# Where the last three steps of a unit's expert selection stand in VectorE's unit loop

## What is computed

```python
v1, i1 = lax.top_k(s1, PEER_TOPK)
v2, i2 = lax.top_k(s2, PEER_TOPK)
cand = (v1[..., :, None] + v2[..., None, :]).reshape(-1, PEER_HEADS, PEER_TOPK * PEER_TOPK)
sc, ci = lax.top_k(cand, PEER_TOPK)
e1 = jnp.take_along_axis(i1, ci // PEER_TOPK, axis=-1)
e2 = jnp.take_along_axis(i2, ci % PEER_TOPK, axis=-1)
eidx = e1 * N_KEYS + e2
gate = jax.nn.softmax(sc, axis=-1)
z = jax.nn.gelu(jnp.einsum('cd,chkd->chk', hc, u_tab[eidx]), approximate=False)
coef = (gate * z.astype(jnp.float32)).astype(hc.dtype)
return jnp.einsum('chk,chkd->cd', coef, v_tab[eidx])
```

## Time and profile before

| | us |
|---|---|
| median of 3 runs | 2758.37 |
| lowest, highest run | 2747.98, 2760.15 |
| the profiled execution | 2752.55 |
| its span (first to last instruction) | 2750.8 |
| DVE busy | 1364.6 (50%) |
| ACT busy | 1031.9 (38%) |
| POOL busy | 1311.3 (48%) |
| PE busy | 1985.1 (72%), granted clock 0.712 of full speed on average |

### The profile page before, as it was taken

One profiled execution on the slowest core, in us unless ns is written; L12 is line 12 of the kernel. 1 busy time (PEld: TensorE's weight loads), 2 busy tenths in 40 slices (PEclk: granted clock), 3 DMA queues, 4 the chain that ended last, 5 costly groups with the idle time before them and its releaser, 6 DMA issues.

```text
span 2750.8 us, 32207 instructions
## 1 busy us (share of the span) xinstructions
PE 1985.1 (72%) x10179; PEld 1594.1 (58%) x10179; DVE 1364.6 (50%) x3386; ACT 1031.9 (38%) x1308; POOL 1311.3 (48%) x1216
## 2 busy tenths in 40 slices
PE   6998865666666665698589897898656666666666
PEld 3676754544545544576389896567444555455455
DVE  1032655465655655323752624726465656556552
ACT  2202344444444444513211111223444444454545
POOL 2000677777777777300000000006777777777774
PEclk8899965565555555799689897899656555555556
DMA  9743899999999999724100002427999999999996
GB/s 359 289 153 124 287 363 329 361 365 367 337 360 351 367 360 392 293 95 168 38 1 1 1 1 76 115 67 249 350 347 361 351 372 347 360 362 364 356 351 243
DMA packets 242654, 717.42 MB, mean 261 GB/s; under 512 B 39672, under 2 KB 45056, under 8 KB 242556
## 3 DMA queue, kind: packets, MB, share of 16 engines
q0 software_dynamic: 165888, 604.05, 59.4%
q1 hardware_dynamic: 62212, 105.00, 10.9%
q10 hardware_dynamic: 14456, 7.06, 1.0%
HBM read 712.38 MB, written 3.65 MB: 260 GB/s over the span
## 4 chain that ended last, share of the span: by engine, by line
PE 35%; DMA 18%; issue 17%; DVE 13%; POOL 10%; ACT 6%; POOLq 0%; DVEq 0%; ACTq 0%; SPq 0%
PE ps L557 14%; DMA ARENA<-in_peer_v,CURV 13%; POOL ARENA L1872 10%; DVE ARENA L1449 7%; PE ps L646 5%; PE ps L774 5%; DMA ARENA<-in_peer_u,CURU 3%; ACT ARENA L1114 2%; ACT L1064 1%; PE ps L534 1%; PE ps L756 1%; PE ps L520 1%; DMA W<-in_w_ada 1%; PE ps L510 1%; PE ps L619 1%
## 5 line engine op out<-in xcount | busy, mean ns | idle before, releaser
L646 PE MATMUL ps<-ident,ARENA 128*128 128x128 f32 x4608 | 1023.3, 398 | 617.5 <-ACT ARENA L1114 616.6
L646 PEld LDWEIGHTS ps<-ident,ARENA 128*128 128x128 f32 x4608 | 833.4, 209 | 807.5 <-ACT ARENA L1114 788.3
L1872 POOL DMA_INDIRECT ARENA<-in_peer_u,CURU x576 | 642.2, 1115 | 1174.2 <-DVE ARENA L1424 978.2
L1114 ACT ACTIVATE ARENA<-ARENA,CF 128x1024 f32<-128x1024 f32 x576 | 658.1, 1147 | 769.8 <-DMA ARENA<-in_peer_v,CURV 766.6
L1449 DVE SCALAR_TENSOR_TENSOR ARENA<-ARENA 128x1024 f32<-128x1024 f32 x576 | 686.6, 1223 | 185.1 <-DMA ARENA<-in_peer_u,CURU 183.5
L1872 POOL DMA_INDIRECT ARENA<-in_peer_v,CURV x576 | 653.1, 1134 | 230.6 <-issue 152.3
L557 PE MATMUL ps<-H,W 128*128 128x288 f32 x1024 | 255.0, 412 | 3.5 <-DVEq L1801 2.8
L1429 DVE TENSOR_REDUCE gsm<-ARENA 128x1 f32<-128x16 f32 x36 | 6.1, 170 | 472.5 <-ACT ARENA L1064 472.5
L557 PEld LDWEIGHTS ps<-H,W 128*128 128x128 f32 x1024 | 197.7, 194 | 58.8 <-DVEq L1801 3.0
L967 ACT ACTIVATE W<-ps 128x512 f32<-128x512 f32 (+2 forms) x97 | 55.8, 577 | 231.4 <-PE ps L774 171.4
L967 ACT ACTIVATE ARENA<-ps 128x512 f32<-128x512 f32 (+4 forms) x106 | 55.0, 541 | 201.7 <-PE ps L557 85.2
(11 more groups left out here) (282 smaller groups left out, 1657.6 us busy)
## 6 DMA issues: line engine op xcount, KB each, us to landing
W<-in_w_ada SPq DMA_DIRECT2D x24, 2048.0 KB, 12.6
W<-in_peer_wq SPq DMA_DIRECT2D x8, 2048.0 KB, 8.2
W<-in_conv_w_in SPq DMA_DIRECT2D x6, 2048.0 KB, 12.3
ARENA<-in_peer_u,CURU POOLq DMA_INDIRECT x576, 6.3
ARENA<-in_peer_v,CURV POOLq DMA_INDIRECT x576, 6.2
W<-in_conv_w_out SPq DMA_DIRECT2D x2, 2048.0 KB, 7.9
W<-in_rwkv_wr SPq DMA_DIRECT2D x2, 2048.0 KB, 24.0
W<-in_rwkv_wk SPq DMA_DIRECT2D x2, 2048.0 KB, 10.4
```

What stands on the lines that cost most here:

```text
L646: m = pe.matmul(ps[:, acc + c // 4, c % 4 * P:(c % 4 + 1) * P], RVV[:, k % RING, c * P:(c + 1) * P], ident[:], start=(first and k == 0 and ...
L1114: act.activation(RVV[:, k % RING, :], RVV[:, k % RING, :], ACT.Copy, scale=CF[:, e, k:k + 1]).then_inc(s_scaled, 1)
L1872: pool.indirect_dma_start(ring[:, k % RING, :], None, tab, bass.IndirectOffsetOnAxis(ap=idx[:, k:k + 1], axis=0)).then_inc(landed[k % RING ...
```

## The change

DVE's unit loop asks for the pieces of the selection at other rows. Before, rows 1 to 7 run two pieces each, which makes all 14; at k = 15 nothing is left. After, rows 1 to 6 run two pieces, row 7 runs piece 13 alone, and piece 14 runs in the loop that empties the generator behind row 15.

```diff
                             if k == 14:
                                 coef(u + 1, 1 - e, 0)
-                            if 1 <= k < 8 or k == 15:
-                                next(chosen, None)
+                            for _ in range(2 * (1 <= k < 7) + (k == 7)):
                                 next(chosen, None)
                     else:
                         coef(u, e, 1)
                     for _ in chosen:
                         pass
```

## The result

| | before | after |
|---|---|---|
| median of 6 runs, us | 2748.48 | 2703.02 |
| lowest to highest | 2739.34 to 2760.15 | 2695.01 to 2708.67 |
| the profiled execution | 2752.55 | 2702.16 |
| its span | 2750.8 | 2700.4 |

The ratio is 0.983, with an interval of 0.980 to 0.985: 45 us faster, where 20 was forecast. In the code of after the lines behind the diff are one lower: the gathers are L1871.

The account below looks back on a forecast made before the run. POOL's issue of 32 gathers a unit was taken as the bound. Per unit, +0.7 us for rows 8 to 15 and -1.36 for CURV's wait net -0.6, -20 us in 32 units: 2758.37 becomes 2739, range 2694 to 2796.

Parts of the forecast that it names:

- POOL's issue bounds the loops: In the unit loops, a unit lasts as long as POOL needs for 32 gathers, 39.7 us with gaps, plus surcharges.
- surcharge: Extra time of POOL's gathers that start while a DVE product row runs: 5.76 us a unit, 0.36 a row.
- The wait at L1429 goes, the three steps are covered: DVE's 472.5 us wait for ACT's exponential vanishes; the three steps, 0.83 us, fit behind row 15 in DVE's idle time.
- CURV's wait goes: At unit boundaries, POOL's v gather no longer waits for CURV: -1.36 us in each of 32 units.
- Rows 8 to 15 at d = 0.42: Surcharge d per product row, for rows coming one by one as they land: 0.42 us, +0.7 us a unit.
- (a): Trace bound for d from rows 0 to 7 with the selection: 0.39 us a row.
- (b): Trace bound for d from layer 1's last unit but one, without selection or wait: 0.60 us a row.
- SP's weights at 0: SP's weights start some 6 us later, behind layer 0's last selection; put at 0, at most 6 us.
- In step: Rival: rows 8 to 15 keep meeting u gathers, d 0.60, +0.8 us a unit, +25 us, 2784; chance 0.31.
- DMA-paced: Rival: DMA sets the rows' pace, d 0.18, -2.6 us a unit, -82 us, 2676; chance 0.10.
- The bandwidth ceiling: Rival: the gathers' bandwidth, 356 GB/s, bounds the unit, so no change, 2758 us; chance 0.06.
- The moved wait: Rival: ACT's exponential falls behind, so L1429 waits behind row 15 and delays the next unit's rows; chance 0.03.

Follow-up runs that it names:

- e8: The kernel after with the write of CURV alone moved back, to ahead of row 15; 2840.43 us, ratio 1.030.
- e3: The kernel after with the product rows reading the tokens' activations from PSUM, copied there by VectorE; 2558.28 us, ratio 0.928.
- e1: The kernel before with only CURV written early, behind row 7's first piece and ahead of the wait; 2754.74 us, ratio 0.999.
- e4: The kernel after with one piece behind each of rows 1 to 9 and two behind rows 10 and 11; 2582.89 us, ratio 0.937.
- e6: The kernel after with one piece behind rows 1 to 11, but two behind rows 7 and 11; 2662.24 us, ratio 0.967.
- e10: The kernel before with CURV written ahead of the wait and the activations read from PSUM; 2571.28 us, ratio 0.934.

## Why the prediction was right, and where it was not

**POOL's issue bounds the loops: right.** That 39.7 us plus surcharge plus idle gives the unit shows nothing by itself, as the three only add up POOL's time. What shows the bound is e8, whose 4.3 us of forced idle time a unit came back as 130 to 137 us. It ends where the surcharge ends: in e3 the landings take over, at 41.1 us a unit.

**The wait at L1429 goes, the three steps are covered: right.** 16.9 us in 4 waits are left of 472.5 in 36, and the steps lie in the landing wait of the next row 0. (In POOL's order u row 15 stands five places behind v row 13, and not four, so there was more room than the 5 us of the prediction.)

**CURV's wait goes, -1.36 us in 32 units: right in size, incomplete in cause.** The idle time fell by 45.0 us in the 30 units of the groups, 1.5 each; in 32 units that is 48, just above the prediction's bounds of 39.5 and 47. But the prediction named CURV alone. e1 shows that row 8's slot stands behind the same wait, and that with CURV early it leaves 1.1 us a unit of idle time (layers 0 and 1). The change frees both, and by e1 it has to.

**Rows 8 to 15 at d = 0.42: the term that was mis-sized.** It was to cost +0.7 us a unit, 22 us in 32 units. Measured, the surcharge is 5.73 a unit on average over both layers, against 5.77: with rows 0 to 7 at 3.1, d is (5.73 - 3.1)/8 = 0.33, what the same rows cost before. Counted gather by gather, each put down to the product row that runs beside it, the surcharge of after is 3.0 for rows 0 to 7 and 2.7 for rows 8 to 15, so 0.34 a row for the latter. The forecast of -20 us becomes (5.73 - 5.76 - 1.36) x 32 = -44 with that, and 45 was measured: the fast end of the forecast's own span, whose d of 0.33 to 0.48 gives -44 to -6 by its sum, where it says -40 to -4. POOL's mean gather stayed at 1.115 us, where the prediction named 1.14. Two thirds of the error was to take (a), 0.39, for the least that a row on its landing costs, though the rows of (a) carry pieces that can make them late; one third was the step towards (b), the in-step unit of the earlier trace rows. In after that unit, from 2605.0 to 2648.1 us, takes 43.1 us where it took 50.6, with no such step:

```profile
2605.00:2648.10 43.10, 29.29 (x130) 23.49 (x129) 22.14 (x47) 19.84 (x19) 33.44 (x32) 0.58 1.00 389
```

(Columns as in the earlier trace rows.) A price seen in a single unit was the state that this unit had fallen into.

**SP's weights at 0:** nothing in the sum needs another value; 46.9 us of the span's 50.4 are in the 30 units, 7.5 in the unit just shown, and some 4 went the other way around them.

**The rivals.** In step did not come. DMA-paced did not come in after, but its state exists: e4 is in it at 0.09 a row, lower than the 0.18 taken from the earlier trace rows. The prediction's condition, the queue full at row 8, was not the one that decides: no row may be late (e6), and the doubled pieces of rows 1 to 6 make rows late. The bandwidth ceiling falls: e3 and e4 hold 410 and 409 GB/s over whole units, on one active core, so 358 GB/s, the figure of the Trainium skill's page SBUF — State Buffer that the prediction weighed, is no cap for this core. The moved wait did not come.

## What to carry to other kernels

When a wait goes, list everything that its engine does behind it and what each consumer needs of that, in the consumer's order: moving one thing out (e1) exposes the next, and only moving the wait itself frees all. Where VectorE works beside gathers issued by GpSimd, feed one input of the long rows from PSUM (e3); if that can't be, keep VectorE's work between two rows shorter than the time between the two landings that they wait for (e4). A busy mean that looks like a fixed price a row (0.36 here) can be the average of two states, one of them nearly free.

## What had not been expected of the hardware

- Rows and gathers settle into a step that one late row ends: 0.09 us of holding a row in e4, 0.28 in e6 (4.56/16), from one row with 3.23 us of DVE work.
- A product row with one input in PSUM takes as long as with both in SBUF (1.21 us in e10, 1.22 in after), and holds nothing.
- The profile's releaser can be another than the cause: POOL's waits for CURV in e8 and for row 8's slot in e1 and e10 stand mostly under PE.
